# The delta rule's states and small inputs loaded in the block of the first norm

## The reference, cut to what matters

```python
z = h @ w_in                                    # combined projection, 3080 columns
beta = sigmoid(z[..., o3:o4])                   # the last 8 columns: 4 for beta, 4 for g
g = -exp(a_log) * softplus(z[..., o4:] + dt_bias)
od, s_new = _gated_delta(q, k, v, g, beta, s0)  # s0: state_delta, 8 samples x 4 heads x 128 x 128
od = _rmsnorm(od, gdn_norm_g) * silu(gate)
```

## Time and profile before

| | |
|---|---|
| median of three runs | 2547.58 us (2545.9 to 2551.32) |
| profiled execution, its own time | 2549.36 us |
| its span | 2547.6 us |
| TensorE (PE) busy | 2061.0 us, 81% |
| VectorE (DVE) busy | 1281.7 us, 50% |
| ScalarE (ACT) busy | 778.5 us, 31% |
| GpSimd (POOL) busy | 645.0 us, 25% |
| mean granted clock of TensorE | 0.913 |
| bytes moved by DMA | 874.97 MB, mean 343 GB/s |
| SP's queue (q1) | 37139 packets, 210.60 MB |

### The profile page before, as it was taken

How to read it: one execution, slowest core, us unless ns; L and a number is a source line. 1 busy time by engine, 2 the same in 40 slices (tenths; PEclk the granted TensorE clock), 3 DMA queues, 4 the chain that set the end, 5 groups by cost and what they waited for, 6 DMA issues and landing times. The chain is left out here.

```text
span 2547.6 us, 25620 instructions
## 1 busy us (share of the span) xinstructions
PE 2061.0 (81%) x9026; PEld 1031.3 (40%) x9026; DVE 1281.7 (50%) x3157; ACT 778.5 (31%) x2275; POOL 645.0 (25%) x645
## 2 busy tenths in 40 slices
PE   7893797478787898877699999987888887988766
PEld 5682685243222243322244464554532222432222
DVE  0084643264677667775511031123556677666754
ACT  1141100024444344443411122121234444344443
POOL 0000000034443444434201000000344434454341
PEclk9985766789999999998799999999899999999978
DMA  5894999679999999999938755753899999999995
GB/s 196 306 339 137 335 331 332 236 268 405 427 427 427 427 427 414 427 426 427 411 147 335 276 200 206 284 199 125 338 426 426 427 427 427 426 423 427 427 427 243
DMA packets 129427, 874.97 MB, mean 343 GB/s; under 512 B 15876, under 2 KB 29700, under 8 KB 45195
## 3 DMA queue, kind: packets, MB, share of 16 engines
q0 software_dynamic: 92160, 662.74, 62.6%
q1 hardware_dynamic: 37139, 210.60, 23.4%
HBM read 861.98 MB, written 118.81 MB: 385 GB/s over the span
## 5 line engine op out<-in xcount | busy, mean ns | idle before, releaser
L1430 PE MATMUL tail_acc<-tail_ring,tail_diag 128*128 128x512 f32 x1216 | 597.7, 622 | 111.5 <-ACT tail_diag L1289 110.6
L1177 DVE CUSTOM_DVE_ANT_0 tail_ring<-tail_ring,all_h 128x1024 f32<-128x1024 f32 x344 | 418.8, 1223 | 235.8 <-DMA tail_ring<-in_peer_uv,tail_idx 235.3
L1430 PE MATMUL tail_acc<-mid_wring,tail_diag 128*128 128x512 f32 x832 | 413.3, 624 | 98.7 <-ACT tail_diag L1289 98.5
L1570 POOL DMA_INDIRECT mid_wring<-in_peer_uv,tail_idx x232 | 239.0, 1030 | 1001.7 <-DVE all_x L1062 525.8
L1570 POOL DMA_INDIRECT tail_ring<-in_peer_uv,tail_idx x344 | 369.4, 1074 | 480.4 <-PE tail_acc L1430 410.8
L1430 PEld LDWEIGHTS tail_acc<-tail_ring,tail_diag 128*128 128x128 f32 x1216 | 217.0, 193 | 477.2 <-ACT tail_diag L1289 297.3
L1177 DVE CUSTOM_DVE_ANT_0 mid_wring<-mid_wring,all_h 128x1024 f32<-128x1024 f32 x232 | 283.3, 1223 | 175.4 <-DMA mid_wring<-in_peer_uv,tail_idx 174.1
L1283 ACT ACTIVATE tail_gelus<-tail_dots 128x1 f32<-128x1 f32 x576 | 116.2, 202 | 723.3 <-DVE tail_dots L1177 723.0
L1430 PEld LDWEIGHTS tail_acc<-mid_wring,tail_diag 128*128 128x128 f32 x832 | 147.8, 193 | 352.6 <-ACT tail_diag L1289 223.9
L1681 PE MATMUL mix_acc<-mid_wring,all_hT 128*128 128x512 f32 x576 | 273.4, 610 | 1.5 <-PEq L80 1.4
L1289 ACT ACTIVATE tail_diag<-all_ident,tail_weights 128x128 f32<-128x128 f32 x512 | 205.5, 401 | 26.4 <-PE tail_acc L1430 9.9
(11 more groups left out here) (363 smaller groups left out, 2099.3 us busy)
## 6 DMA issues: line engine op xcount, KB each, us to landing
mid_wring<-in_w_qkv SPq DMA_DIRECT2D x18, 2048.0 KB, 8.8
out_kv_s<-in_cache_kv_w SPq DMA_DIRECT2D x8, 4064.0 KB, 49.2
mix_ring<-in_kT POOLq DMA_DIRECT2D x16, 1024.0 KB, 8.1
mix_ring<-in_v_rows POOLq DMA_DIRECT2D x16, 1024.0 KB, 10.3
ab_ring_w<-in_w_in_ab SPq DMA_DIRECT2D x6, 2048.0 KB, 11.4
mix_ring<-in_kT POOLq DMA_DIRECT2D x16, 768.0 KB, 9.3
mix_ring<-in_v_rows POOLq DMA_DIRECT2D x16, 768.0 KB, 9.0
mid_wring<-in_w_out SPq DMA_DIRECT2D x4, 2048.0 KB, 10.4
```

The costliest lines, as they stand in the source:

```text
L1177: V.tensor_tensor_reduce(out=u, in0=u, in1=h[:, g, :], scale=1.0, scalar=0.0, op0=ALU.mult, op1=ALU.add, accum_out=dots[:, n:n + 1]).then_ ...
L1430: last = mm(acc[g][:, c * 512:(c + 1) * 512], diag[:, n % DIAGS, :], v[:, c * 512:(c + 1) * 512], start=first, stop=final)
L1570: pool.indirect_dma_start(slot(r), None, table, bass.IndirectOffsetOnAxis(ap=idx[:, j, i:i + 1], axis=0)).then_inc(landed[r], 16)
```

## The change

The seven tensors of the delta rule that are loaded from HBM (gate weights, masks, owner, a_log, dt_bias, norm gain, sample states S0) are allocated in the outer phase of layer 0, with one semaphore, by the new function `delta_inputs`. The 14 loads are given to `first_norm_phase` as the list `later`, and SP issues them there behind `ahead`. `delta_phase` issues none of them; its first SP instructions are the eight cache copies of window 2048. TensorE's wait is the same, on the new semaphore. The kernel's diff, whole:

```diff
--- before.py
+++ after.py
@@ -147,7 +147,7 @@
 
 
 
-def first_norm_phase(nc, K, T, hT, ahead):
+def first_norm_phase(nc, K, T, hT, ahead, later):
 
     x, xs, h, hs = K["x"], K["xs"], K["h"], K["hs"]
     with ExitStack() as ctx:
@@ -166,6 +166,8 @@
                 sp.dma_start(gain[:], broadcast_rows(T["norm_mix"][0:1, :], D)).then_inc(gain_in, 16)
                 sp.dma_start(gain_s[:], T["gain_s"][0]).then_inc(gain_in, 16)
                 for to, frm, landed in ahead:
+                    sp.dma_start(to, frm).then_inc(landed, 16)
+                for to, frm, landed in later:
                     sp.dma_start(to, frm).then_inc(landed, 16)
 
             @block.vector
@@ -566,7 +568,22 @@
 
 
 
-def delta_phase(nc, name, K, T, hT, zT, conv, mixT, cache_out):
+def delta_inputs(P, T):
+
+    G = {"cst": P.sb("masks", [128, 12, 128]), "own": P.sb("owner", [128, DEC_B]), "wab": P.sb("w_ab", [128, KC, 8]),
+         "alog": P.sb("a_log", [128, 4]), "dtb": P.sb("dt_bias", [128, 4]), "gn": P.sb("norm_gain", [128, 1]),
+         "S0": P.sb("S_sample", [128, DEC_B, 4, 128])}
+    loaded = P.sem("delta_loaded")
+    loads = [(G["wab"][:], T["w_in_ab"][0].rearrange("(k p) n -> p k n", p=128)[:, :, IN_AB - 8:IN_AB], loaded),
+             (G["cst"][:], T["c_gdn"].rearrange("p (k n) -> p k n", k=12), loaded),
+             (G["own"][:], T["c_owner"], loaded), (G["alog"][:], broadcast_rows(T["a_log"], 4), loaded),
+             (G["dtb"][:], broadcast_rows(T["dt_bias"], 4), loaded),
+             (G["gn"][:], T["gdn_norm_g"].rearrange("a n -> n a"), loaded)]
+    loads += [(G["S0"][:, b, :, :], T["state_delta"][0, b].rearrange("h k v -> k h v"), loaded) for b in range(DEC_B)]
+    return G, loaded, loads
+
+
+def delta_phase(nc, name, K, T, G, loaded, hT, zT, conv, mixT, cache_out):
 
 
 
@@ -601,10 +618,7 @@
 
     with ExitStack() as ctx:
         P = Phase(nc, ctx, name)
-        cst = P.sb("masks", [128, 12, 128])
-        own = P.sb("owner", [128, DEC_B])
-        wab = P.sb("w_ab", [128, KC, 8])
-        alog, dtb, gn = P.sb("a_log", [128, 4]), P.sb("dt_bias", [128, 4]), P.sb("norm_gain", [128, 1])
+        cst, own, wab, alog, dtb, gn, S0 = (G[k] for k in ("cst", "own", "wab", "alog", "dtb", "gn", "S0"))
         ab, gt = P.sb("ab", [128, 3, 8]), P.sb("g_tmp", [128, 3, 4])
         beta, g = P.sb("beta", [128, 3, 4]), P.sb("g", [128, 3, 4])
         per_tile = lambda name, shape: [P.sb(f"{name}{t}", shape) for t in range(3)]
@@ -618,12 +632,11 @@
         Rv, Rk, kd = per_tile("Rv", [128, 4, 128]), per_tile("Rk", [128, 4, 128]), P.sb("k_decay", [128, 3, 4, 128])
         u, wT, qe = P.sb("u", [128, 3, 4, 128]), P.sb("wT", [128, 3, 4, 128]), P.sb("q_exp", [128, 3, 4, 128])
         S, vn, vs = P.sb("S", [128, 4, 128]), P.sb("v_new", [128, 4, 128]), P.sb("v_new_s", [NS, 4, 128])
-        S0 = P.sb("S_sample", [128, DEC_B, 4, 128])
         wS, vm = P.sb("wS", [128, 4, 32]), P.sb("v_owner", [32, DEC_B, 128])
         oT, ones = P.sb("oT", [128, 4, NTOK]), P.sb("ones", [128, 128])
         sqr = P.sb("sqr", [128, 4, NTOK])
         bank = [P.ps(f"bank{i}", [128, 512]) for i in range(8)]
-        loaded, dve_steps, act_steps, stored = (P.sem(s) for s in ("loaded", "dve_steps", "act_steps", "stored"))
+        dve_steps, act_steps, stored = (P.sem(s) for s in ("dve_steps", "act_steps", "stored"))
         turn = {"gates": P.sem("gate_turn"), "main": P.sem("main_turn")}
         turn.update({t: P.sem(f"tile{t}_turn") for t in range(3)})
         heads = [b[:].rearrange("q (h c) -> q h c", h=4) for b in bank]
@@ -654,16 +667,6 @@
         with nc.Block() as block:
             @block.sync
             def _(sp):
-                sp.dma_start(wab[:], T["w_in_ab"][0].rearrange("(k p) n -> p k n", p=128)[:, :, IN_AB - 8:IN_AB]
-                             ).then_inc(loaded, 16)
-                sp.dma_start(cst[:], T["c_gdn"].rearrange("p (k n) -> p k n", k=12)).then_inc(loaded, 16)
-                sp.dma_start(own[:], T["c_owner"]).then_inc(loaded, 16)
-                sp.dma_start(alog[:], broadcast_rows(T["a_log"], 4)).then_inc(loaded, 16)
-                sp.dma_start(dtb[:], broadcast_rows(T["dt_bias"], 4)).then_inc(loaded, 16)
-                sp.dma_start(gn[:], T["gdn_norm_g"].rearrange("a n -> n a")).then_inc(loaded, 16)
-                for b in range(DEC_B):
-                    sp.dma_start(S0[:, b, :, :], T["state_delta"][0, b].rearrange("h k v -> k h v")
-                                 ).then_inc(loaded, 16)
                 roll_cache(sp, T, 2, cache_out)
                 sp.wait_ge(turn["main"], at["main", "c3 S dve"] + 1)
                 sp.dma_start(T["out_delta_p"][0, 0].rearrange("h k v -> k h v"), S[:]).then_inc(stored, 16)
@@ -2244,17 +2247,18 @@
 
         with ExitStack() as c2:
             P0 = Phase(nc, c2, "l0")
+            G, delta_loaded, delta_loads = delta_inputs(P0, T)
             zT, conv = P0.sb("zT", [128, 24, NTOK]), P0.sb("conv", [128, 12, NTOK])
             with ExitStack() as c3:
                 W = WeightRing(Phase(nc, c3, "ab_ring"), T["w_in_ab"][0], IN_AB - 8, 3)
-                first_norm_phase(nc, K, T, hT, W.start)
+                first_norm_phase(nc, K, T, hT, W.start, delta_loads)
                 def copies(sp):
                     roll_cache(sp, T, 0, cache_out)
                     roll_cache(sp, T, 1, cache_out, range(2))
 
                 columns_phase(nc, "ab", hT, T["w_in_ab"][0], IN_AB - 8, zT, ahead=W, after=copies)
             conv_phase(nc, "cv", K, T, zT, mixT, conv, cache_out)
-            delta_phase(nc, "gd", K, T, hT, zT, conv, mixT, cache_out)
+            delta_phase(nc, "gd", K, T, G, delta_loaded, hT, zT, conv, mixT, cache_out)
 
         with ExitStack() as c2:
             P1 = Phase(nc, c2, "mid")
```

## The result

The changed kernel takes 2551.7 us (median of 19 runs, 2546.73 to 2559.21), the kernel before 2546.65 us in runs beside them (19 runs, 2540.92 to 2553.96). The ratio is 1.002, 95% interval 1.001 to 1.0029: slower by 5 us, with an interval of about 2.5 to 7.4. The forecast was 7.5 us slower. The profiled execution took 2553.16 us for a span of 2551.4.

What follows compares the result with a forecast made beforehand. Many small pieces bound the kernel; the prize was 14.0 us of idle core at the delta loads, in a block DMA bounds. Terms +17.8 + 0.5 + 0.2 - 11.0 = +7.5 us gave 2555.1 us, range 2549 to 2562.

Steps and rivals of the forecast that it cites:

- the limit of the queue: SyncE's issues, first norm and delta block: held until about 2500 packets are left, whatever their size.
- the delta block: Layer 0's delta block: DMA bounds it; without the loads the copies start earlier, -11.0 us, bounds -9.8 and -13.9.
- SyncE in the first norm: First norm: 14 issues behind the weight loads hold SyncE until 38.3, delaying the projection by 17.8 us; bounds +6.0 and +22.2.
- The clock: Projection's start: after longer TensorE idling, 4.5 us at half speed instead of 3.4, +0.5 us; bounds 0 and +1.8.
- The extra clear and barrier: Leaving the outer phase, which now owns a semaphore: one more clear and barrier, +0.2 us.
- Compute in the delta block: Delta block: compute moves forward by 14.0 us against the block's start, VectorE's end from 458.85 to 444.9.
- rival 2: Delta block: copies leave early enough that compute bounds it, -13.9 instead of -11.0; net +4.6, 2552.2 us; chance 0.12.
- the signs named ahead: Changed profile: first-norm issues end near 38, product near 39, seams unchanged, a store wait closing delta 3 to 6 us after VectorE.
- the first (SyncE not held, 2543.0): First norm: SyncE is not held, +6.0 there; net -4.6, 2543.0 us; chance 0.10.
- The third (held to the last landing, 2560.7): First norm: SyncE held until the last load lands, +22.2, copies gain only 9.8; net +13.1, 2560.7 us; chance 0.12.

Runs made afterwards that it cites:

- second and third run: Changed kernel with the eight state loads (second) or the six small loads (third) issued in the projection's block instead; one execution each, 2544.61 and 2549.13 us.
- fourth run: Changed kernel with one of eight window-2048 cache copies issued at the end of the convolution's SP list: 2542.52 us, ratio 0.998 to the kernel before.
- the split wait: Kernel before, loads unmoved; TensorE starts after the six small loads and waits for the states where first read: 2553.12 against 2552.07 us, ratio 1.0004.
- a moved copy: One window-2048 copy issued at the convolution's end: on the changed kernel 2542.52 us; on the kernel before 2538.2 against 2552.07 us, ratio 0.9942.
- the second profile: Kernel before, unchanged, profiled once more: this execution took 2550.50 us.

## Why the prediction was right, point by point

The forecast was +7.5 us, the runs gave +5.05, and the range held it. Sign and mechanism were right; two sizes, the limit of the queue and the delta block, agree with the runs by luck in part, as said below. The terms came out so:

- **SyncE in the first norm: +17.8 forecast, +14.7 measured.** The mechanism was right: the block ended with SyncE's last issue. The size was off in the landing, "by 30.0 + 12.7 = 42.7". The 12.7 us came from the delta block, where the loads were issued onto an empty queue and the transfer in part waited for the issues (the earlier trace rows has slices of 50 to 70 GB/s). Behind a full queue the same data took about 10 us, from 28.3 to 38.3, at some 310 GB/s. The last issue ended 3.3 us before the data instead of 4.4. The step "the same count from packets of two sizes is why I take it for the limit" was a miscount. The trace of the kernel before has 2477 packets left at 16.60, but 1024 of them belong to the issue that ended there, so 1453 stood in front of it; at 248.87 it has 1704 left, not 2500 (the 4.4 us run on to TensorE's start, past the last data), and 512 of them are that issue's own, so 1192 stood in front. In the changed kernel 1771 were left when the last issue ended (35.05). What the second and third run bear out is the kind of limit, elements in front and not bytes, at some 1440 to 1540 of them. It does not cover the stores behind the copies: the earlier trace rows has a hold with fewer, and what holds those stays open.
- **The clock: +0.5 forecast, +0.1 measured.** The first output group took 41.86 - 35.90 = 5.96 us against 5.84. One execution does not settle this term. In the three other kernels that leave TensorE idle there for 10 to 16 us, the first group took 6.70 to 7.05 us (7.05 in the fourth run, whose front is that of the changed kernel); in the five other profiles without that idle time it took 4.15 to 5.96. So the longer idle time may well make the start dearer by 1 us or more.
- **The extra clear and barrier: +0.2 forecast, +0.3 in the profile.** From the last store's landing (460.28 + 3.8) to the next issue it is 1.2 us against 0.8 (461.3 to 462.17).
- **The delta block: -11.0 forecast, -10.5 between the two profiles.** That DMA closes it was right: the changed kernel waits 13 us after VectorE, the split wait bought nothing, and a moved copy bought 9 to 14 us. The split of the sum was off, though its total fitted: in the earlier trace rows the copies are through at about 451, not 453.6, and the stores need 10 us, not 7.5. And the block of the kernel before is not one number: 223.1 in the profile I worked from, 226.5 in the second, 227.6 with the split wait. The four kernels with the loads out of it and all eight copies in it lie between 211.7 and 212.5. Measured against the second profile the gain would be 14 us, at the edge of my bounds; that the two profiles differ by just the forecast is in part luck.
- **Compute in the delta block: -14.0 forecast, -20.5 seen** (VectorE's end 219.8 after the block's start, now 199.3). 14.2 of it is the removed wait. The rest goes with TensorE's pace in the one execution I worked from: from TensorE's start to VectorE's end it took 205.5 us, the nine other profiled executions 199.1 to 202.3. Over the same first 704 product instructions, before and after (start and end, length, busy time of TensorE's two sides, VectorE, ScalarE and GpSimd, granted clock, DMA share, GB/s):

```profile
253.30:393.60 140.30, 117.53 (x704) 105.13 (x704) 79.43 (x195) 9.97 (x20) 0.00 (x0) 0.70 1.00 337
252.70:386.60 133.90, 112.11 (x704) 99.59 (x704) 79.85 (x198) 11.26 (x21) 0.00 (x0) 0.73 1.00 334
```

  These instructions kept TensorE busy for 5.4 us less, at a higher granted clock. It did not count, since the block ends with DMA; rival 2, which wanted compute to close it, is refuted by the store wait that still does.
- **What I had not priced**: the convolution's length between the ten profiled executions with the same compute instructions, 116.5 to 121.5 us.

Of the signs named ahead, two failed: SyncE's issues ended at 35, not near 38, and the store wait closes the block 13 us after VectorE, not 3 to 6, because compute moved forward by 20.5 us and the copies by 10.5.

Of the rivals, the first (SyncE not held, 2543.0) was refuted by the two issues of 5 us. The Trainium skill ("DMA: Bandwidth & Descriptors", "Anatomy of one DMA") says that many descriptors can be emitted before their cost shows; but that section is about transfers issued from GpSimd, and I applied it to SyncE's. In this kernel SyncE was held for 5 us at once, with the queue full. The third (held to the last landing, 2560.7) is refuted by the 3.3 us between SyncE's end and the data's. The second (compute closes the block, 2552.2) comes nearest to the measured time, but its mechanism is the one that is refuted.

## What to carry to other kernels

Moving a load earlier also moves its issue. In this kernel an issue behind a full queue held the issuing engine for about 5 us at a time; where a block's end waits for that engine, the hold lands on every engine. Put such issues into the first block that has other work for longer than the hold lasts: here the projection's block, which issued them 5 us later, turned +5 us into about -11. And before removing a wait, find what closes the block behind it: halving the visible wait gave nothing, while moving one copy into idle DMA time gave 14 us without touching any load.

## What the runs showed of the hardware

- The hold of an issue follows the elements in front of it: 4.85 to 4.90 us right behind three loads of 1024 elements of 2 KB, whether the held load had 1024 elements of 32 B or 512 of 512 B. The next issue was held 5.00 us behind the former and 2.44 us behind the latter. These issues ended with 1445 to 1538 elements in front of them still to come.
- The same load set took 12.7 us from an empty queue and about 10 us behind a full one.
- Eight stores of 256 KB were issued in 5.00 us with the copies drained (fourth run), and in 29.49 us behind them (changed kernel).
